# One hybrid layer on one core: recurrence levels merged over both directions, and an expert ring of 16 chunks in place of 12

## The reference

```
mod = cond @ w_mod + b_mod                       # six modulation rows per group
h   = rmsnorm(x) * (1 + sc1) + sh1
parts = split(h @ w_in)                          # 13 windows of 256 columns
att = attention (8 heads)                        # dense for context, 2-D window + cache for sample
rec = HGRN2 recurrence, forward and backward     # 4 heads
        a[t,s] = sum_k q[t,k] * k[s,k] * exp(b[t,k] - b[s,k])   for s <= t (backward: s >= t)
        o = a @ v + q*exp(b) @ state
mlp = u * (ws @ rmsnorm(v) + bs)                 # chunked gating
x  += g1 * concat(att, rec, mlp) @ w_out
h2  = rmsnorm(x) * (1 + sc2) + sh2
x  += g2 * sum over the top 4 of 32 experts of gate_e * (((up + 1) * glu) @ w_down_e + b_down_e)
y   = rmsnorm(x) * final_g
```

## Time and profile before

| | us |
|---|---|
| median of three executions | 1190.43 (1189.28 to 1190.52) |
| the profiled execution, its own time | 1188.43 |
| its span, first to last instruction | 1186.6 |
| PE busy / DVE / ACT / POOL in the span | 1141.7 / 237.7 / 161.4 / 23.1 |
| mean granted TensorE clock | 0.994 |
| DMA over the span | 455.38 MB, 384 GB/s |

### The profile page before, as it was taken

The page is one execution under the profiler, slowest core; times in us unless marked ns, Lnnn a source line. Parts: engine busy times, 40 slices in busy tenths (PEclk is TensorE's granted clock), DMA queues, the critical chain, the costliest instruction groups (busy, mean ns, idle before and its releaser), DMA issues.

```text
span 1186.6 us, 13428 instructions
## 1 busy us (share of the span) xinstructions
PE 1141.7 (96%) x5470; PEld 543.5 (46%) x5470; DVE 237.7 (20%) x471; ACT 161.4 (14%) x285; POOL 23.1 (2%) x43
## 2 busy tenths in 40 slices
PE   7899999999999999999999999999999999999996
PEld 2689955454444444444444343434343434343432
DVE  2435762421111010101010101010101010102023
ACT  1222341210101010101010101011010101010001
POOL 0400000000000000000000000000000000000000
PEclk9999989999999999999999999999999999999998
DMA  9996367749999999999999999999999999999994
GB/s 326 331 357 234 115 223 294 280 185 427 423 429 427 430 428 429 427 430 427 429 429 429 429 428 429 428 429 427 430 427 430 427 430 427 430 427 430 426 422 166
DMA packets 54827, 455.38 MB, mean 384 GB/s; under 512 B 5199, under 2 KB 18531, under 8 KB 27798
## 3 DMA queue, kind: packets, MB, share of 16 engines
q1 hardware_dynamic: 51648, 446.46, 91.0%
q0 software_dynamic: 2080, 6.98, 1.8%
q10 hardware_dynamic: 1078, 1.65, 0.6%
HBM read 453.36 MB, written 1.70 MB: 384 GB/s over the span
## 4 chain that ended last, share of the span: by engine, by line
PE 80%; ACT 2%; DVE 2%; DMA 2%; issue 0%; DVEq 0%; ACTq 0%
PE bank L1535 55%; PE bank L1492 11%; PE sums L1548 5%; PE bank L1515 3%; PE bank L1400 2%; DMA ring<-in_w_up 2%; ACT k_pool L654 2%; PE bank L1580 1%; ACT colsT L640 1%; PE bank L1198 1%; PE sums L1198 1%; PE bank L1470 0%; PE sums L1434 0%; PE sums L1554 0%; PE bank L1205 0%
## 5 line engine op out<-in xcount | busy, mean ns | idle before, releaser
L1535 PE MATMUL bank<-ring,colsT 128*64 128x512 f32 x2048 | 446.5, 593 | 0.1
L1535 PEld LDWEIGHTS bank<-ring,colsT 128*64 128x64 f32 x2048 | 145.5, 137 | 296.8 <-issue 294.7
L1535 PE MATMUL bank<-ring,k_pool 128*64 128x512 f32 x1024 | 226.8, 595 | 14.9 <-ACT k_pool L654 14.9
L1535 PEld LDWEIGHTS bank<-ring,k_pool 128*64 128x64 f32 x1024 | 70.7, 137 | 149.6 <-issue 127.9
L1048 DVE TENSOR_SCALAR k_pool<-bank 128x512 f32<-128x512 f32 x32 | 22.1, 691 | 584.4 <-PE bank L1535 584.4
L1492 PEld LDWEIGHTS bank<-keyT,rows 128*128 128x128 f32 x512 | 121.9, 328 | 24.7 <-issue 23.5
L1492 PE MATMUL bank<-keyT,rows 128*128 128x128 f32 x512 | 128.0, 403 | 0.3 <-ACT colsT L640 0.3
L1548 PE MATMUL sums<-d_pool,colsT 64*128 64x512 f32 x256 | 63.6, 615 | 0.0
L1057 DVE TENSOR_SCALAR k_pool<-bank 128x512 f32<-128x512 f32 x32 | 22.1, 691 | 151.4 <-PE bank L1535 151.4
L1246 PE MATMUL bank<-colsT,ring 128*128 128x256 f32 x224 | 49.6, 380 | 2.9 <-DMA ring<-in_w_in 2.1
L650 ACT ACTIVATE k_pool<-k_pool 128x512 f32<-128x512 f32 x32 | 20.2, 630 | 224.1 <-DVE k_pool L1048 224.1
(11 more groups left out here) (308 smaller groups left out, 543.8 us busy)
## 6 DMA issues: line engine op xcount, KB each, us to landing
ring<-in_w_gate SPq DMA_DIRECT2D x58, 2048.0 KB, 15.2
ring<-in_w_up SPq DMA_DIRECT2D x58, 2048.0 KB, 18.3
ring<-in_w_down SPq DMA_DIRECT2D x58, 2048.0 KB, 15.4
ring<-in_w_mod SPq DMA_DIRECT2D x24, 1024.0 KB, 11.2
ring<-in_w_in SPq DMA_DIRECT2D x13, 1024.0 KB, 12.6
ring<-in_w_gate SPq DMA_DIRECT2D x12, 1024.0 KB, 9.2
ring<-in_w_up SPq DMA_DIRECT2D x12, 1024.0 KB, 10.4
ring<-in_w_down SPq DMA_DIRECT2D x12, 1024.0 KB, 11.6
```

Source lines behind the costliest of these rows:

```text
L1535: ins = mm(bank[CAP * half:CAP * (half + 1), :], lhsT(2 * r + kk), w[:, kk, 512 * half:512 * (half + 1)], start=m == 2 and r == 0 and kk = ...
```

## The change

Four things change together.

1. **Levels.** `level_qk`, `level` and `level_store` handle both directions in one call. Queries and keys of both directions share one buffer per level (each half of a block belongs to one direction), in two alternating buffers (`Ql`, `Kl`). PE does eight 64-row matmuls per level in the form of `diagonal`. A level is now wholly behind one projection, and the first stands behind Q_0. `level_exp` and the DVE list move up to match; the store of level 6 goes before the gating of the chunked MLP. The zeroing by POOL goes away.
2. **Masks.** 8 masks of uint8 (128 KB) are loaded straight into `masks`; the cast goes away.
3. **Ring.** The ring has 16 slots for the experts. The last four lie over `kv_pool`, `hq_hi`, `tmp`, `q_start`, `biasN`, `cv`, `ckT` and `wsT`. The first loads into them wait until the residual is added (`x1_ready` at 4). Four experts are three turns of the ring, so SP's loop and PE's loop take four experts per iteration (PE: 7 iterations of two pairs each, and two pairs written out behind them).
4. **Small moves.** `mbias` moves to the buffer of g1, and its load waits for `x1_ready` instead of `cat_ps`; the final residual uses `at_pool` as its scratch.

```diff
 RING = 12
+EXPERT_SLOTS = 16
+EXPERT_CHUNKS = 12
...
-    m = np.zeros((P, 16, P), np.float32)
+    m = np.zeros((P, 8, P), np.uint8)
...
-        same = s // (2 * w) == t // (2 * w)
-        first, second = s % (2 * w) < w, t % (2 * w) >= w
-        m[:, n] = same & first & second
-        m[:, 7 + n] = m[:, n].T
-    m[:, M_DIAG] = s == t
+        m[:, n] = (s // (2 * w) == t // (2 * w)) & (s // w != t // w)
...
-        ring = sb("ring", RING * SLOT).rearrange("p (s w) -> p s w", s=RING)
+        ring_cols = sb("ring", EXPERT_SLOTS * SLOT)
+        ring = ring_cols.rearrange("p (s w) -> p s w", s=EXPERT_SLOTS)
+        late = ring_cols[:, RING * SLOT:EXPERT_SLOTS * SLOT]
...
+        kv_pool = late[:, 0:3072]
+        hq_hi = late[:, 3072:4096]
...
+        tmp = late[:, 4096:5120]
...
+        q_start = late[:, 6144:6656]
...
+        biasN = late[:, 5120:6144].rearrange("p (h k) -> p h k", h=NH)
+        cv = late[:, 6656:7168]
+        ckT = late[:, 7168:7680].rearrange("p (h l) -> p h l", h=HP)
+        wsT = late[:, 7680:8192].rearrange("p (g t) -> p g t", g=GM)
...
-        Kl = k_pool[:, 0:1024].rearrange("p (d n) -> p d n", d=2)
-        Qpair = gain.rearrange("p (d a q n) -> p d a q n", d=2, a=4, q=2)
+        Kl = k_pool[:, 0:1024].rearrange("p (o n) -> p o n", o=2)
+        Ql = gain.rearrange("p (o n) -> p o n", o=2)
...
-        mbias = kv_pool[0:2 * NE, 0:D]
+        mbias = g12[0:2 * NE, 0:D]
...
+        expert_order = [(AT_MOE + n) % RING for n in range(RING)] + list(range(RING, EXPERT_SLOTS))
...
+        def pair_slot(u, b):
+            return expert_order[2 * ((6 * u + b) % PAIR_SLOTS)]
...
+        def pair_loads(group, u, b):
+            return (group * 3 + ((6 * u + b) // PAIR_SLOTS + 1)) * 16 + mixer_loads(pair_slot(u, b))
...
+            def load_pair(e, u, b):
+                w = (w_gate, w_up, w_down)[b // 2]
+                slot = pair_slot(u, b)
+                sp.dma_start(ring[:, slot:slot + 2, :].rearrange("p s (k n) -> p (s k) n", k=2),
+                             w[0, bass.ds(e, 1), 512 * (b % 2):512 * (b % 2 + 1), :]
+                             .rearrange("a (p k) n -> p (a k) n", p=P)).then_inc(slot_loaded[slot], 16)
+            def load_expert(group, u):
+                for b in range(6):
+                    sp.wait_ge(chunks_used, group * 48 + (EXPERT_CHUNKS * u + 2 * b + 2 + AT_MOE - EXPERT_SLOTS))
+                    load_pair(group * 4 + u, u, b)
...
+            def load_expert_by_halves(e):
+                for b in range(6):
+                    n = 6 * e + b
+                    w = (w_gate, w_up, w_down)[b // 2]
+                    for half in range(2):
+                        slot = pair_slot(e % 4, b) + half
+                        if slot >= RING and n < PAIR_SLOTS:
+                            sp.wait_ge(ev("x1_ready"), 4)
+                        else:
+                            sp.wait_ge(chunks_used, AT_MOE + 2 * n + half + 1 - (RING if n < 6 else EXPERT_SLOTS))
+                        sp.dma_start(ring[:, slot, :].rearrange("p (k n) -> p k n", k=2),
+                                     w[0, e, 512 * (b % 2):512 * (b % 2 + 1), :]
+                                     .rearrange("(p o k) n -> p o k n", o=2, k=2)[:, half]).then_inc(slot_loaded[slot], 16)
 
             for e in range(2):
...
-            small_load("masks_loaded", k_pool, const_masks)
+            small_load("masks_loaded", masks.rearrange("p m t -> p (m t)"), const_masks)
...
-            pool.wait_ge(ev("masks_ready"), 1)
-            nc.gpsimd.memset(Kl, 0.0).then_inc(ev("k_zero"), 1)
             pool.wait_ge(ev("h_ready"), 4)
-            nc.gpsimd.memset(gain, 0.0).then_inc(ev("k_zero"), 1)
             small_load("norm2_loaded", gsc, bcast_row(b_mod[0:1, 4 * D:5 * D]))
...
-            pool.wait_ge(ev("cat_ps"), 4)
+            pool.wait_ge(ev("x1_ready"), 4)
...
             copy_win(K_0)
+            level_exp(0)
             copy_win(Q_0)
-            level_exp(0)
+            level_exp(1)
             copy_win(K_1)
-            level_exp(1)
+            level_exp(2)
...
-            level_exp(2)
+            level_exp(3)
...
-            level_exp(3)
+            level_exp(4)
             copy_win(V_1)
-            level_exp(4)
+            level_exp(5)
...
-            level_exp(5)
...
-            dve.wait_ge(ev("masks_loaded"), 16)
-            V.tensor_copy(masks.rearrange("p m t -> p (m t)"), k_pool).then_inc(ev("masks_ready"), 1)
...
-                    V.tensor_tensor(Qpair[hd, d, :, q, :].rearrange("p a (n m) -> p a n m", m=w),
-                                    Dl[hd, d, :].rearrange("p (a n h m) -> p a n h m", a=4, h=2, m=w)[:, :, :, 1 - d, :],
-                                    hqT[hd, :].rearrange("p (a n h m) -> p a n h m", a=4, h=2, m=w)[:, :, :, 1 - d, :],
...
+                K, Q = level_view(Kl[:, n % 2], w), level_view(Ql[:, n % 2], w)
+                dve.wait_ge(ev("lvl_exp"), 4 * n + 4)
+                if n != 1:
+                    dve.wait_ge(ev("lvl_mm"), max(1, n))
+                for d in range(2):
+                    x = level_view(Dl[:, d, :], w)
+                    V.tensor_tensor(Q[:, :, 1 - d, :], x[:, :, 1 - d, :], level_view(hqT, w)[:, :, 1 - d, :], ALU.mult).then_inc(ev("lvl_qk"), 1)
+                    V.tensor_tensor(K[:, :, d, :], x[:, :, d, :], level_view(keyT[:, d, :], w)[:, :, d, :], ALU.mult).then_inc(ev("lvl_qk"), 1)
...
-                    V.copy_predicated(AT[:, q, :].rearrange("p (a n h m) -> p a n h m", a=4, h=2, m=w)[:, :, :, 1 - d, :],
-                                      level_view(masks[:, 7 * d + n, :], w)[:, :, 1 - d, :].unsqueeze(1).to_broadcast([P, 4, 64 // w, w]),
-                                      B[2 + d].rearrange("p (a q n m) -> p a q n m", a=4, q=2, m=w)[:, :, q]).then_inc(ev("lvl_store"), 1)
...
+                    V.copy_predicated(AT[:, q, :].rearrange("p (a t) -> p a t", a=4),
+                                      masks[:, n, :].unsqueeze(1).to_broadcast([P, 4, P]),
+                                      B[2 + q].rearrange("p (a t) -> p a t", a=4)).then_inc(ev("lvl_store"), 1)
...
+            def hgrn_level(n):
+                level_qk(n)
+                dve.wait_ge(ev("lvl_qk"), 4 * n + 4)
+                if n + 1 < len(LEVELS):
+                    level_diff(n + 1)
...
-            hgrn_level(0, 0)
-            hgrn_level(0, 1)
             diagonal_store()
+            hgrn_level(0)
...
-                for d in range(2):
-                    level_store(n - 1, d)
-                    hgrn_level(n, d)
-                if n == 2:
+                level_store(n - 1)
+                hgrn_level(n)
+                if n == 3:
...
+                    level_store(6)
...
-                    buf = kv_pool[:, 1024 + 512 * q:1024 + 512 * (q + 1)]
+                    buf = at_pool[:, 512 * (q % 2):512 * (q % 2 + 1)]
...
-            def level(n, d):
-                pe.wait_ge(ev("lvl_qk"), 6 * n + 3 * d + 3)
-                pe.wait_ge(ev("lvl_store"), max(2, 4 * n + 2 * d))
+            def level(n):
+                pe.wait_ge(ev("lvl_qk"), 4 * n + 4)
+                pe.wait_ge(ev("lvl_store"), 2 * n + 2)
                 for m in range(4):
-                    ins = mm(B[2 + d][:, P * m:P * (m + 1)], Kl[:, d, P * m:P * (m + 1)], Qpair[:, d, m],
-                             start=True, stop=True)
+                    for q in range(2):
+                        hd = slice(HD * q, HD * (q + 1))
+                        ins = mm(B[2 + q][:, P * m:P * (m + 1)], Kl[hd, n % 2, P * m:P * (m + 1)],
+                                 Ql[hd, n % 2, P * m:P * (m + 1)], start=True, stop=True)
                 ins.then_inc(ev("lvl_mm"), 1)
 
-            def project_with_levels(i, n):
-                project(i, between=lambda: level(n - 1, 1))
-                level(n, 0)
+            def project_with_level(i, n):
+                project(i)
+                level(n)
...
             project(K_0)
-            project(Q_0)
             pe.wait_ge(ev("early_out"), 3)
             diagonal()
-            project(K_1)
-            level(0, 0)
-            project_with_levels(Q_1, 1)
+            project_with_level(Q_0, 0)
+            project_with_level(K_1, 1)
+            project_with_level(Q_1, 2)
 
             pe.wait_ge(ev("win_out"), K_1 + 1)
             for h in range(HP):
                 ins = tr(B[6][:, P * h:P * (h + 1)], kT[:, h, 0, :], ident)
             ins.then_inc(ev("kout_ps"), 1)
-            project_with_levels(V_0, 2)
+            project_with_level(V_0, 3)
...
-            def product(bank, m, lhsT, count, tokens=None, after=None, by_chunks=0):
+            def product(bank, m, lhsT, group, u, tokens=None, after=None, loads=pair_loads, halves_of=None, each_half=False):
...
+                    if half == 0:
+                        pe.wait_ge(slot_loaded[slot], loads(group, u, b))
+                    if halves_of is not None and half == each_half:
```

(6 more changed lines are left out.)

174 lines of the change are left out of this document (67 added, 107 removed).

## The result

The changed kernel took 1178.35 us (median of four runs, 1177.7 to 1180.4), the kernel before 1189.9 beside it: a ratio of 0.9907, 95% interval 0.989 to 0.9924. In a second set of six runs the median was 1178.33 (ratio 0.9911, 0.9892 to 0.993). The forecast was 1178.4. The profiled execution of after took 1177.7 us (span 1175.9), that of before 1188.4.

What follows compares the result with a forecast made beforehand. PE's chain was taken as the bound (58.04 us a pair, DMA 58.73). Terms -4.3 + 0.4 - 1.4 - 3.3 - 2.1 - 0.3 = -11.0 took the profiled 1188.4 to 1177.4; with half of 2.0 added, median 1178.4, range 1175.0 to 1185.0.

Steps and rivals of the forecast that it cites:

- Levels on PE: Mixer levels: 14 direction calls of 0.90 us become seven merged calls of 1.19 us; -4.3 us, bounds -5.0 to -3.6.
- Levels on DVE and ACT: Level work on DVE and ACT is covered except ahead of level 4, where PE stalls anew: +0.4 us (0 to 0.8).
- Behind the levels: After the last level, projection H_G covers DVE's end work, so PE's two waits go: -1.4 us.
- The clock: Behind the levels, the 6.83 us stretch at half clock returns to full clock once the two waits go: -3.3 us.
- Masks: Early mixer: the mask load shrinks from 1024 to 128 KB, so the 2.12 us wait for w_in goes: -2.1 us.
- The ring: Expert stage: four more chunks give each load 9.8 us more, so PE never waits for a landing: -0.3 us.
- mbias: Ahead of the experts: its loads, issued later at about 223.6 us, still land before PE wants them: 0 us.
- From the profiled execution to the median: Median before is 2.0 us above its profile; half was taken as late landings that the longer ring removes.
- Rival 1: Behind the levels the clock falls all the same: 1181.7 us; chance 0.17 alone, 0.09 together with the early wait.
- 2 (early wait): Early mixer: other small loads take the masks' place and the wait stays: 1180.5 us; chance 0.14 alone.
- 4: Only the levels' arithmetic gains; clock and early wait stay, DVE's waits move rather than go: 1186.2 us; chance 0.05.
- 3 (a loop that must be fetched): Expert loop: PE fetches its longer body anew at each of six jumps, 4 us each: 1202.4 us; chance 0.06.

Runs made afterwards that it cites:

- waits: The changed kernel with six memsets on VectorE delaying Kend and Qend, and the last level's store behind Qend again; 1186.12 us.
- waits_filled: The kernel of waits, with unread 128x512 matmuls on PE: 7 ahead of its wait behind the levels, one ahead of each of the last three w_mod waits; 1184.8 us.
- body4: The changed kernel with PE's expert loop unrolled to four pairs (about 2180 instructions, 3 passes) and four pairs written out behind it; 1189.9 us.
- ring12: The changed kernel with an expert ring of 12 slots instead of 16; 1179.62 us.
- split12: The changed kernel on 12 slots, aT in two banks copied half by ScalarE, half by VectorE, a pair's second biases behind the down product; 1180.74 us.
- order12: The changed kernel on 12 slots, with activations turned and copied ahead of the gather and the second biases; 1179.56 us.
- order16: The changed kernel on 16 slots, with activations turned and copied ahead of the gather and the second biases; 1168.7 us, ratio to before 0.9828.
- the two split kernels: The changed kernel with aT's copy split between ScalarE and VectorE and second biases behind the down product: 16 slots 1178.58 us, 12 slots 1180.74 us.

## Why the prediction was right

**Levels on PE** (forecast -4.3; bounds -5.0 to -3.6). From K_0 to the modulation sums 6.44 us are gained. Less the two waits (1.41) and the 0.6 of slow clock ahead of the sums, 4.4 are left; with the new stall added, the calls gave 4.6. The price of a call held: 1.09, and the projection behind it 7.10 instead of 7.00, so 1.19, though the 0.1 sits behind the call and not ahead of it.

**Levels on DVE and ACT** (+0.4). The stall ahead of level 4 is there, in the place named: V_1 would have ended at 112.59 + 7.10 = 119.69, the call starts at 119.87. It is 0.18 us. Three products overlap by 0.09 each, which the sum of four times 0.43 left out.

**Behind the levels** (-1.4). Both waits are gone; DVE is done with Kend and Qend at 145.2, PE wants them at 149.95.

**The clock** (-3.3). 0.6 ahead of the sums and 2.76 from the sums to the biases: -3.36. It was the least certain term, and the experiments on the waits show that the reason was right as well. The Trainium skill, "TensorE: Matmul & The Clock Gate", section "Loop structure matters more than you think", shows that long waits for a DMA between matmuls let PE run on the slow clock. The pair waits and waits_filled agrees (0.53 and 1.00 in the sums' stretch), and here two waits for VectorE of 2.13 us in all were enough.

**Masks** (-2.1). In the profiled pair the part from the first project to K_0 gives -2.4, in the medians the megabyte alone is worth 1.5. The cause was right (the landing did move), the pricing was not: the DMA time of the megabyte (2.15 us) fitted the wait of one profile (2.12), while the landing moved by 4 us or more, and the wait that it removes varies with the start.

**The ring** (-0.3). The link at 1076.55 is gone, but the expert stage grew by 0.28 us: every second pair takes 0.085 us more, between the second biases and the down product, where the sum said that nothing was added that PE sees. In the medians the ring is worth 1.3 us, within their spread. The loads keep a lead of 9.2 us at the least in the profile (landed at 1078.56, used at 1087.75), where before's shrank to nothing; that is close to what was worked out from 4 slots (9.8). The loads of w_up land 3 us sooner than before (11.7 and 19.5 us), and those of w_down 3 us later (14.6 and 22.4 in the two windows, 11.1 and 19.5 before).

**mbias**: PE did not wait for it; the biases follow the gather without a gap.

**From the profiled execution to the median.** Here a step failed and the number survived. The 2.0 us between the profiled execution of before and its median were read as late landings in the experts, half of which the ring would remove. The second profile of before shows another cause: half clock in the start stage, and a longer wait for w_in with half clock behind it; its last pair, 58.59 us where the first profile has 58.37, is only 0.2 us longer. Even that is a part only: of the 45 timed runs of before beside the three sets, the 24 with a mean granted clock of 0.995 or more have a median of 1188.9 us, the other 21 one of 1189.9, in a spread from 1186.2 to 1194.6. What makes up the rest was not found. The start added 1.1 us to the profiled execution of after, and its median lies only 0.6 above it, not 1.0.

**Luck.** Between the profiled executions 10.7 us are gained where the sum says 11.0. The 1.1 us lost in the start were not forecast. They are nearly made up by small gains: the calls gave 0.3 more than was put down, the stall cost 0.2 less, the early mixer gave 0.3 more. In the ring's term the longer pairs (+0.3 instead of -0.3) were hidden by the 0.5 us at the very end, which are not the ring's. So the mechanisms were right, but that the time agrees to 0.1 us is luck.

**The rivals.** Rival 1 (clock) fell in both profiles of after, behind the levels. 2 (early wait) fell. 4 fell with them. 3 (a loop that must be fetched) fell for 1090 instructions and is true for 2180. It was priced at 4 us a jump; the two jumps of body4 cost 4.2 and 5.7, about 2.5 of each a gap and the rest the clock behind it. The Trainium skill, "Runtime: NRT & Kernel Launch", section "Instruction fetch mechanics", gives PE an instruction memory of 2048 and a window of two blocks (512) for branches. The first as the limit of a loop fits the runs, the second does not: 543 and 1090 instructions looped without a packet of q8, 2180 did not.

## What to carry to other kernels

When two resources are within 1 or 2% of each other, write down the pace of both (here 58.04 and 58.73 us) and the lead that the buffer holds between them. A deeper buffer is worth the length of the lead and not a rate, and only once the faster side has been made faster: about 1 us by itself here, 10.9 with the shorter order (9.6 between the two profiled executions). Price a wait of PE with the half clock that can follow it, which here cost more than the wait (2.1 us of waits, 3.5 of clock). And unroll a hardware loop with an eye on the instructions in its body.

## What the runs showed of the hardware

- PE's granted clock fell to 1.2 GHz in four places, each in or right behind an idle of PE: the waits for w_mod at the start (worth 1.1 to 1.3 or 2.2 us), a wait of 3.06 us for w_in (1.7 us), waits of 0.86 and 0.55 us behind the levels (3.3 us), and the gaps of 2.46 and 2.68 us in body4. In the two kernels that filled the waits it fell nowhere but at the very end. The start is the same in all other kernels, yet the clock falls there in seven of twelve profiles and not in five: an idle of 1.5 us can bring the half clock and need not.
- The 16 DMA engines bring 25.17 MB in 58.73 us, 428.6 GB/s, and hold this to 0.01 us a pair in four kernels (ring12, split12, order12, order16). The Trainium skill, "DMA: Bandwidth & Descriptors", section "Where 436 GB/s comes from", puts the ceiling of the ports at 435 GB/s, and says that for loads from HBM the HBM side binds at about 358. The traces, of a kernel on one core, come within 1.5% of the first and lie above the second.
- At the DMA pace a deeper ring lengthens a load's way: from issue to landing of w_up 22.8 us with 12 slots (order12) and 29.7 with 16 (order16), at the same 58.73 us a pair. A long way from issue to landing alone does not say that a load is late.
- Every second pair takes 0.085 us more (0.15 in the two split kernels) in the kernels with the ring of 16 and PE's waits for aT, in none with the ring of 12, and not in order16, where the copy of aT is hidden. In body4 the 2nd, 6th, 10th and 12th pairs have it, but not the 14th, which stands behind the loop with constants in the place of the loop's register; in after, where the 14th is in the loop, it has it. That would fit waits that PE computes from its loop register between aT and the down product. But the ring of 12 computes them as well and doesn't show it, so the cause stays open.
